# Three operand buffers of TensorE begin 48, 80 and 112 bytes behind multiples of 128 in SBUF

## The reference, cut to what matters

```python
def first_block(x, ...):
    for l in range(2):
        h = einsum('bsd,de->bse', x, w_in[l])           # 1024 -> 9216 columns
        o_a, o_b, o_c = retention(...), chunk_attention(...), diff_attention(...)
        merged = g0 * (o_a @ w_branch_a[l]) + g1 * (o_b @ w_branch_b[l]) + g2 * (o_c @ w_branch_c[l])
        x = layer_norm(ALPHA * x + merged @ w_out[l], ln1_g[l], ln1_b[l])
        u_gate, u_up = split(x @ w_ffn_in[l], 2)        # 2 x 2816 columns
        x = layer_norm(ALPHA * x + (silu(u_gate) * u_up) @ w_ffn_out[l], ln2_g[l], ln2_b[l])

def second_block(x, ...):
    for l in range(2):
        x = layer_norm(ALPHA * x + 0.5 * swiglu(x, ffn1_...), ...)
        proj = x @ w_in[l]
        mix = concat([short_conv(...), gmlp(...), nsa_attention(...)]) @ w_out[l]
        x = layer_norm(ALPHA * x + mix, ...)
        x = layer_norm(ALPHA * x + 0.5 * swiglu(x, ffn2_...), ...)
```

## Time and profile before

| | |
|---|---|
| median of 3 runs | 2027.65 us |
| lowest and highest | 2027.23 and 2028.76 us |
| the profiled execution, its own time | 2028.55 us |
| its span in the profile | 2026.5 us |
| granted TensorE clock in it | 0.999 |
| TensorE busy | 2010.0 us of 14176 matmuls |
| VectorE busy | 1274.6 us |
| ScalarE busy | 927.0 us |

### The profile page before, as it was taken

The page is one execution under the profiler, slowest core; times in us unless marked ns, Lnnn a source line. Parts: engine busy times, 40 slices in busy tenths (PEclk is TensorE's granted clock), DMA queues, the critical chain, the costliest instruction groups (busy, mean ns, idle before and its releaser), DMA issues.

```text
span 2026.5 us, 32504 instructions
## 1 busy us (share of the span) xinstructions
PE 2010.0 (99%) x14176; PEld 1835.6 (91%) x14176; DVE 1274.6 (63%) x1844; ACT 927.0 (46%) x1275; POOL 32.2 (2%) x56
## 2 busy tenths in 40 slices
PE   8999999999999999999999999999999999999998
PEld 7888999999887999999999989799999998979997
DVE  6566666555756665655665567765566556776555
ACT  4445444444545444544444454454444445445442
POOL 0000000000000000000000000000000000000000
PEclk9999999999999999999999999999999999999999
DMA  8544555666544555586556646458656664555663
GB/s 287 168 149 132 187 172 168 199 207 190 167 163 136 167 168 186 147 261 187 167 181 188 185 135 167 105 157 251 187 167 188 187 188 134 158 136 157 189 188 101
DMA packets 416133, 352.51 MB, mean 174 GB/s; under 512 B 28816, under 2 KB 361080, under 8 KB 415992
## 3 DMA queue, kind: packets, MB, share of 16 engines
q1 hardware_dynamic: 415992, 350.44, 57.3%
HBM read 349.36 MB, written 1.05 MB: 173 GB/s over the span
## 4 chain that ended last, share of the span: by engine, by line
PE 94%; DVE 3%; ACT 2%; issue 0%; DMA 0%; DVEq 0%; SPq 0%
PE ps L201 29%; PE ps L202 29%; PE ps L203 29%; PE ps L1446 2%; PE ps L1527 2%; PE ps L1565 1%; DVE hl L1990 1%; PE ps L1599 1%; ACT hl L1749 1%; DVE er L2157 0%; DVE small L2116 0%; ACT er L1841 0%; PE ps L1637 0%; DVE er L2114 0%; PE ps L1570 0%
## 5 line engine op out<-in xcount | busy, mean ns | idle before, releaser
L1990 DVE TENSOR_TENSOR hl<-raw,hl 128x1024 fp32r<-128x1024 f32 (+2 forms) x555 | 756.3, 1393 | 393.5 <-ACT hl L1749 392.5
L201 PE MATMUL ps<-xt,hl 128*128 128x256 f32 (+1 forms) x2672 | 753.5, 282 | 0.0
L202 PE MATMUL ps<-xt,hl 128*128 128x256 f32 (+1 forms) x2672 | 746.0, 279 | 0.0
L203 PE MATMUL ps<-xt,hl 128*128 128x256 f32 (+1 forms) x2672 | 745.5, 279 | 0.0
L1749 ACT ACTIVATE hl<-raw 128x2048 fp32r<-128x2048 f32 (+1 forms) x323 | 612.8, 1899 | 183.6 <-PE ps L203 169.4
L201 PEld LDWEIGHTS ps<-xt,hl 128*128 128x128 f32 (+1 forms) x2672 | 501.0, 187 | 4.7 <-issue 1.5
L202 PEld LDWEIGHTS ps<-xt,hl 128*128 128x128 f32 (+1 forms) x2672 | 500.9, 187 | 3.2
L203 PEld LDWEIGHTS ps<-xt,hl 128*128 128x128 f32 (+1 forms) x2672 | 500.8, 187 | 0.2
L201 PE MATMUL ps<-hl,o 128*128 128x512 f32 x656 | 261.9, 399 | 0.0
L203 PE MATMUL ps<-hl,o 128*128 128x512 f32 x656 | 259.4, 395 | 0.0
L202 PE MATMUL ps<-hl,o 128*128 128x512 f32 x656 | 259.4, 395 | 0.0
(11 more groups left out here) (202 smaller groups left out, 1605.8 us busy)
## 6 DMA issues: line engine op xcount, KB each, us to landing
raw<-in_w_in SPq DMA_DIRECT2D x83, 1024.0 KB, 5.1
raw<-in_w_ffn_in SPq DMA_DIRECT2D x88, 512.0 KB, 5.2
raw<-in_ffn_gate SPq DMA_DIRECT2D x88, 512.0 KB, 4.0
raw<-in_ffn_up SPq DMA_DIRECT2D x88, 512.0 KB, 5.3
raw<-in_ffn_down SPq DMA_DIRECT2D x44, 1024.0 KB, 5.0
raw<-in_w_ffn_out SPq DMA_DIRECT2D x22, 1024.0 KB, 5.0
raw<-in_w_out SPq DMA_DIRECT2D x12, 1024.0 KB, 5.1
raw<-in_w_branch_a SPq DMA_DIRECT2D x8, 1024.0 KB, 4.9
```

Of the source, the lines that this page charges most:

```text
L201: e.matmul(out, l[0], r[0], start=start, stop=False)
L202: e.matmul(out, l[0], r[1], start=False, stop=False)
L203: return e.matmul(out, l[1], r[0], start=False, stop=stop)
L1990: e.tensor_tensor(lo[:, c], m["raw"][:, k % NRAW, 0:n][:, c], hi[:, c].bitcast(F), ALU.subtract).then_inc(s.low.up(("low", k), *([("low", ...
```

## The change

The three buffers are allocated 16 bytes longer and are used from their fifth element on. Shape, order and strides of the views are as they were, and every engine's list of instructions and waits is the same.

```diff
-            "x": sb("xs", [128, 2, D]), "xt": sb("xt", [128, 2, 8, S], R),
-            "o1": sb("o1", [128, 2, 8, S], R), "o2": sb("o2", [128, 2, 4, S], R), "gb": sb("gb", [128, 2, D]),
+            "x": sb("xs", [128, 2, D]), "xt": sb("xt", [128, 4100], R), "o1": sb("o1", [128, 4100], R), "o2": sb("o2", [128, 2052], R), "gb": sb("gb", [128, 2, D]),
...
         m = {k: v[:] for k, v in m.items()}
+        for name, n in (("xt", 8), ("o1", 8), ("o2", 4)):
+            m[name] = m[name][:, 4:4 + 2 * n * S].rearrange("p (z k t) -> p z k t", z=2, k=n)
```

## The result

The changed kernel takes 2040.97 us (median of four runs, 2039.78 to 2041.71); the kernel before takes 2027.85 us (median of four runs beside them, 2027.23 to 2028.76). The ratio is 1.0063, with a 95% interval from 1.0050 to 1.0076: slower by 13.1 us. The time lies within the predicted range of 2012 to 2044 us, but outside the 2024 to 2031.5 us that went with the likeliest case A: the forecast of no effect was wrong, and what came about is close to rival B.

The account below looks back on a forecast made before the run. The prediction took TensorE's matmul paces to bound the kernel, busy for 2010.0 of 2026.5 us. Its four parts, each priced 0, left the span at 2026.5 us, forecast as the median of 2027.7 us, range 2012 to 2044 us.

Parts of the forecast that it names:

- case A: Whole kernel: the change has no effect, 2027.7 us, own range 2024 to 2031.5 us; chance 0.62.
- rival B: 256-column streams: the slower variant becomes the rule through the operands' relative position, 1.67 ns more each, +14.6 us, 2042 us; chance 0.14.
- Part 3: VectorE and ScalarE writes into the three buffers: 0 on the path, at the most some hundredths.
- part 4: Tensors behind `o2`, moved by 96 bytes to remainders that some tensor had before: 0.
- Part 1: 8784 TensorE matmuls with moving rows of `xt`, `o1`, `o2`: priced at 0, bounds 32.0 us up and 14.6 us down.
- D: 256-column streams: a better relative position lets the pace fall towards 115.0 ns, -14.6 us, 2013 us; chance 0.15.
- Rival C: 256-column streams: one 32-byte granule more each, 120.3 ns instead of 116.7, +32.0 us, 2060 us; chance 0.09.
- Part 2: Loads of stationary pieces of `xt`, `o1`, `o2`, hidden behind streams: 0, at most 3.6 us up and 1.7 us down.

Follow-up runs that it names:

- e5: Against the kernel before, `hl` begins at byte 400 by 512 instead of 384, and `xt`, `o1`, `o2` at 176 instead of 160: 2026.22 us, ratio 0.9992.
- e11: Against the kernel before, start bytes by 512 set to 400 for `hl`, 336 for `xt`, 176 for `o1` and `o2`: 1992.31 us, ratio 0.9825.
- e1: Against the kernel before, the three buffers stay in place and only what lies behind `o2` moves by 96 bytes: 2028.21 us, ratio 0.9999.
- e10: Against the kernel before, `xt` begins at byte 64 by 512, `o1` and `o2` at 368, with `hl` still at 384: 2014.25 us, ratio 0.9933.
- e12: Against the kernel before, only `xt` moves, by 8 bytes, to byte 168 by 512: 2048.35 us, ratio 1.0100.
- e4: Against the kernel before, `hl` slots at bytes 384, 400, 416 by 512, and `xt`, `o1`, `o2` at 288, 336, 368: 2036.97 us (one run).
- e9: Against e4, same places, but feature blocks between a product's first and last load and compute 32 columns instead of 128: 2018.73 us (one run).
- e3: Against the kernel before, `xt`, `o1`, `o2` all at remainder 112 by 128 (bytes 240, 368, 496 by 512): 2009.42 us, ratio 0.9906.

## Why the prediction was right and wrong

**What bounds the kernel: right.** TensorE's paces are the time. Kernels with the same instructions spread from 1992 to 2048 us; the idle time ahead of the 512-column streams of line 201 past `xt`, the largest that TensorE has ahead of any of its large groups, stays at 2.0 to 2.7 us in all of them, and the sums of distances give each difference to within 1 us where I took them (the change, e5, e11).

**Part 3 (writes) and part 4 (what lies behind): right.** Line 2104 took 425 ns in the changed kernel, line 1829 418 ns, as the earlier trace rows had them, and e1 puts part 4 at 0, with an interval of 0.1% or 2 us to either side.

**Part 1 (moving rows), priced at 0: wrong.** It measured +13.3 us (12.3 of `xt`, 1.0 of `o1` and `o2`). The step that failed is the one that drew independence from the earlier trace rows: 233.3 ns for 512 columns with a moving operand at remainder 0, 116.7 for 256 columns at remainder 32, the one twice the other, hence no effect of the start. Those are two different forms with different stationary operands, and both numbers belong to one set of places. e5 shows that each moves on its own: the 512 columns fell to 226.7 while the 256 rose to 118.3. The ratio of two was a coincidence of the places before. That the time still fell into the range is owed to rivals B and D, which the range was widened to hold.

**The sign that was there and was weighed too low.** The earlier trace rows had 118.3, 117.5 and 116.7 ns for streams of one length, and I wrote that such variants are not set by the address, since one pair of operands showed two of them. e10 shows what that was: for one pair of places two steady states can exist. It does not say that places don't matter. Nor did the two paces of the earlier trace rows belong to one pair of places: in one the row of `xt` moves past `hl`, in the other `hl` past `xt`. With that read rightly, the three paces for no visible reason stand against A, and 0.62 for A was too much.

**The formula of the page was read too narrowly.** The prediction says that 7.5 and 17.5 ns of each matmul have no source that the Trainium skill's page "TensorE: Matmul & The Clock Gate" (Back-to-back issue gap) names. The section gives N/2.4 + 2.5 ns as the gap of an isolated matmul, and says that in a stream of load and matmul pairs the spacing is set by both. So it does name the load beside the stream, though it has no figure for 256 columns.

**Rival B: its size was right, its mechanism in part.** +1.67 ns on 8784 matmuls was to give 14.6 us; `xt` rose by 1.5 ns (116.8 to 118.3), 12.3 us. But B and D had all three buffers go the same way by their relative position; in fact `xt` got B, `o1` more than that and `o2` got D (113.3, below the 115.0 that I took for the floor). `xt` has 7968 of the 8736 matmuls with 128 stationary columns, so its draw decided the sign. And the relative position alone is refuted by e5.

**Rival C: refuted.** Starts 16 bytes off a multiple of 32 are at 113.3 ns as well as at 120.0 (240 and 208). The memory lines of 16 bytes of the Trainium skill's page "SBUF — State Buffer" (Specifications (TRN2)), which the prediction weighed for A, don't explain the result either: all starts but that of e12 are multiples of 16, and the time still moves by -1.75% to +0.7% among them.

**Part 2 (stationary pieces), priced at 0: right in this change by luck.** The 3024 long streams stayed within 0.3 us, because past 176, 208 and 240 with `hl` at 384 they happen to keep about 233 ns. In e10, with `hl` still at 384 and other places of the three buffers, the same streams took 15 us less, more than the whole change. That a load has 233.3 ns to hide in and is therefore worth 0 took for granted that the stationary piece has no other way to act on the stream.

**What the mechanism is, and what stays open.** Shown is that the places of both operands set the pace. Not shown, but the likeliest reading: the reading of the stationary columns for the next matmul and the stream of the moving operand get in each other's way in SBUF, by where both lie. For it speak that both places count (e4, e5) and that with a short load, though also with a narrower output, the stream is faster at two of three places of the weights (e9). Against it as the whole story stand the first slot of e9, slow even with the short load, and the matmuls with 24 stationary columns: they too depend on the place, from 113.8 ns in the changed kernel over 115.0 before to 117.9 in e12. The Trainium skill's page "TensorE: Matmul & The Clock Gate" (Step-by-step: what each phase is for) gives TensorE two independent read ports and says that loading the next weights takes no read bandwidth from the running matmul. If it is the load that e9's fall from 120.0 to 113.9 ns comes from, e9 doesn't agree with that for these operands. Not settled: the rule from two places to a pace, its period, why the first matmuls of a stretch run at another pace, and why the entry into a stretch goes with one of two paces in e10. That the choice goes with the step into the stretch and comes out alike in the next layer makes DMA writes into `raw` at the same time a less likely cause, but with other traffic it wasn't tried.

## What to carry to other kernels

Where TensorE is busy for 99%, the bytes at which its two operands begin are worth -1.75% to +1.0% with not one instruction changed. No rule for them came out of these runs, but they can be measured cheaply: put the slots of one operand at different offsets in one kernel and read 24 to 72 starts of each stretch. Then time the chosen set as a whole, since a pace read in a sweep need not come back: the set of e11 came within 5 us of its forecast, that of e10 missed it by 28. An edit that changes a length or an order of allocations ahead of such a buffer can move the time by as much as the edit was meant to bring, so hold the places fixed when comparing, and look at the pace of each form, since in e5 two shifts of 12.5 and 17.5 us hid in an unchanged time.

## What the runs showed of the hardware

- A stream of 256 columns of `float32r` has a steady pace of 113.3 to 120.0 ns at a granted clock of 0.999, depending on the places of both operands; one of 512 columns about 227 to 234.
- A stretch can begin at one pace and fall into another after 4 (e11) to 12 (e3) matmuls, and one pair of places can have two that last (117.8 and 113.3 in e10). There the pace goes with how the stretch is entered: 49 of 49 stretches that begin 226 or 227 ns after the last long matmul are slow, 7 of 7 that begin 230 to 236 ns after it are fast.
- A shift of 8 bytes changes the pace as well: 119.2 ns in e12, where its neighbours 8 bytes to either side have 116.8 and 118.3.
- With 24 stationary columns the pace depends on the places too: 113.8 ns (changed), 115.0 (before), 117.9 (e12).
